# Four units at once behind the norms: the feature tile as the outer loop, with their low parts on GpSimd

## What is computed

```python
x = x + g_a[:, None, :] * rms_norm(y, attn_post_norm)
h = modulate(rms_norm(x, ffn_pre_norm), sh_f, sc_f)        # norm "x1"
u = h @ w_up                                               # the up projection, 2048 -> 2 x 5632
u = conv_b + sum(up[:, t:t + S] * conv_w[t] for t in range(3))
gate, val = split(u, 2);  y = (gelu(gate) * val) @ w_down
x = x + g_f[:, None, :] * rms_norm(y, ffn_post_norm)
h = rmsnorm(x, norm_g_2)                                   # norm "x2"
proj = h @ w_in_2                                          # the second projection, 2048 -> 48 tiles of 128
```

## Time and profile before

| | |
|---|---|
| median of three runs | 1979.6 us |
| the profiled execution's own time | 1982.76 us |
| its span | 1981.0 us |
| TensorE matmul busy | 1784.0 us, 90% of the span |
| VectorE, ScalarE, GpSimd busy | 1224.9 (62%), 855.4 (43%), 296.1 us (15%) |
| split of a half, high part, on ScalarE | 1057 ns, 512 times |
| low part of a half on VectorE | 1233 ns, 448 times |
| low part of a half on GpSimd | 2665 ns, 64 times |

### The profile page before, as it was taken

One profiled execution on the slowest core, in us unless ns is written; L12 is line 12 of the kernel. 1 busy time (PEld: TensorE's weight loads), 2 busy tenths in 40 slices (PEclk: granted clock), 3 DMA queues, 4 the chain that ended last, 5 costly groups with the idle time before them and its releaser, 6 DMA issues.

```text
span 1981.0 us, 33453 instructions
## 1 busy us (share of the span) xinstructions
PE 1784.0 (90%) x13960; PEld 1715.3 (87%) x13960; DVE 1224.9 (62%) x1745; ACT 855.4 (43%) x1384; POOL 296.1 (15%) x190
## 2 busy tenths in 40 slices
PE   1289798797997999999999999999699999988997
PEld 1289797696996999999999999999599999966797
DVE  8255788936467766766766756655654446556544
ACT  2244333453344544544544535434444443455442
POOL 8834233000443000000000000000200000042000
PEclk8589799988997999999999999999999999988999
DMA  9178768723792665766766655554245554431041
GB/s 387 71 254 318 286 242 296 264 95 117 258 344 101 232 217 194 231 211 202 230 205 214 226 191 185 176 171 163 83 142 187 183 181 160 159 118 65 25 173 59
DMA packets 102821, 377.11 MB, mean 190 GB/s; under 512 B 11536, under 2 KB 11664, under 8 KB 102544
## 3 DMA queue, kind: packets, MB, share of 16 engines
q1 hardware_dynamic: 102672, 374.99, 54.6%
HBM read 372.85 MB, written 2.10 MB: 189 GB/s over the span
## 4 chain that ended last, share of the span: by engine, by line
issue 43%; PE 39%; DVE 10%; POOL 5%; ACT 1%; DMA 1%; SPq 0%; DVEq 0%; ACTq 0%; POOLq 0%
PE ps L509 10%; PE ps L510 10%; PE ps L511 10%; POOL masks L1655 4%; DVE ada_acc L1171 3%; DVE probs L1282 1%; PE ps L540 1%; DVE stats L1256 1%; PE ps L591 1%; POOL probs L1648 1%; PE ps L547 1%; PE ps L625 1%; PE ps L610 1%; DVE w_lo L1156 1%; ACT w_hi L858 1%
## 5 line engine op out<-in xcount | busy, mean ns | idle before, releaser
L509 PE MATMUL ps<-h_hi,w_hi 128*128 128x256 f32 x3264 | 944.8, 289 | 27.4 <-DVE w_lo L1156 7.9
L510 PE MATMUL ps<-h_lo,w_hi 128*128 128x256 f32 x3264 | 931.3, 285 | 0.0
L511 PE MATMUL ps<-h_hi,w_lo 128*128 128x256 f32 x3264 | 931.0, 285 | 0.0
L1156 DVE TENSOR_TENSOR w_lo<-raw,w_hi 128x1024 fp32r<-128x1024 f32 x448 | 552.0, 1233 | 414.5 <-ACT w_hi L858 412.5
L858 ACT ACTIVATE w_hi<-raw 128x1024 fp32r<-128x1024 f32 x512 | 538.8, 1057 | 441.5 <-PE ps L511 410.7
L509 PEld LDWEIGHTS ps<-h_hi,w_hi 128*128 128x128 f32 x3264 | 633.8, 194 | 34.1 <-issue 13.4
L510 PEld LDWEIGHTS ps<-h_lo,w_hi 128*128 128x128 f32 x3264 | 634.8, 194 | 1.1
L511 PEld LDWEIGHTS ps<-h_hi,w_lo 128*128 128x128 f32 x3264 | 634.3, 194 | 0.0
L1171 DVE SCALAR_TENSOR_TENSOR ada_acc<-raw,c_act,ada_acc 128x1024 f32<-128x1024 f32 x180 | 243.0, 1381 | 0.7 <-DMA raw<-in_ada 0.4
L1661 POOL TENSOR_TENSOR w_lo<-raw,w_hi 128x1024 fp32r<-128x1024 f32 x64 | 170.1, 2665 | 439.6 <-ACT w_hi L858 439.6
L509 PE MATMUL ps<-g_hi,w_hi 128*128 128x256 f32 x704 | 200.3, 284 | 3.7 <-DVE g_lo L1492 3.7
(11 more groups left out here) (197 smaller groups left out, 1385.5 us busy)
## 6 DMA issues: line engine op xcount, KB each, us to landing
raw<-in_weights SPq DMA_DIRECT2D x512, 512.0 KB, 3.7
raw<-in_ada SPq DMA_DIRECT2D x192, 512.0 KB, 5.1
x<-in_x SPq DMA_DIRECT2D x1, 2048.0 KB, 16.4
out_y<-x SPq DMA_DIRECT2D x4, 512.0 KB, 2.7
consts<-in_consts SPq DMA_DIRECT2D x1, 863.5 KB, 6.3
params<-in_params SPq DMA_DIRECT2D x1, 589.5 KB, 4.2
probs<-in_pos_q SPq DMA_DIRECT2D x1, 128.0 KB, 2.2
probs<-in_pos_k SPq DMA_DIRECT2D x1, 32.0 KB, 1.9
```

Of the source, the lines that this page charges most:

```text
L509: nc.tensor.matmul(out, wh, hi[:, k, :], start=start, stop=False)
L510: nc.tensor.matmul(out, wh, lo[:, k, :], start=False, stop=False)
L511: last = nc.tensor.matmul(out, wl, hi[:, k, :], start=False, stop=stop)
L1156: V.tensor_tensor(w_lo[:, h % W_SLOTS, :], raw[:, raw_slot("w", h), :], w_hi[:, h % W_SLOTS, :].bitcast(F32), ALU.subtract).then_inc(lo_dv ...
```

## The change

The first four units of the up projection and of the second projection run together: h tile n is the outer loop, the four units the inner one, each in a bank of its own. The weight stream of these units is reordered on the host to fit, so a half holds two h tiles of four units, and half 0 is done only when two h tiles have met four units. The banks follow cycles of five and four in place of four and three, the tokens' transposes use other banks, and one of them waits for an earlier copy. The low parts of halves 4 to 11 of both stages go from VectorE to GpSimd. ScalarE's splits of halves 4 to 8 move in between the tiles of h_high, those of 9 to 11 behind it. The two first pairs split no halves of their own but the last one, and the `ada` items 160 and 161 go ahead of them.

```diff
+TOGETHER = 4
+def tile_at(u, n):
+    for first in (U_FF, U_IN2):
+        if first <= u < first + TOGETHER:
+            return UNIT_FIRST[first] + TOGETHER * n + u - first
+    return UNIT_FIRST[u] + n
...
+        elif U_FF <= u < U_IN2:
+            cycle, n = [0, 1, 4, 5, 2], u - U_FF
         elif U_IN2 <= u < U_CMP:
-            cycle, n = [0, 1, 5], u - U_IN2
+            cycle, n = [2, 0, 1, 5], u - U_IN2
...
 POOL_HALVES = set(range(1, N_IN, 2)) | set(range(N_IN + 1, 2 * N_IN, 2)) | set(range(H_O, H_FF, 2)) | set(
-    range(H_CMP + 2, H_OUT2 + 4))
+    range(H_FF + 4, H_FF + 12)) | set(range(H_IN2 + 4, H_IN2 + 12)) | set(range(H_CMP + 2, H_OUT2 + 4))
...
+        TOK_BANKS = [2, 3, 4, 5, 2, 3, 4, 5, 3, 4, 3]
...
+            def units_together(u, hi, lo, arriving):
+                for n in range(KT):
+                    pe.wait_ge(arriving[0], arriving[1] + n + 1)
+                    for j in range(TOGETHER):
+                        t = tile_at(u + j, n)
+                        if n == 0:
+                            bank_free(u + j)
+                        if t % TILES == 0:
+                            pe.wait_ge(*lo_done(t // TILES))
+                        product(t, ps[:, BANK[u + j], 0:S], n, hi, lo, n == 0, n == KT - 1)
...
-                        pe.wait_ge(tok_copied, i - 3)
-                    bank = SCORE + i % 4
+                        pe.wait_ge(tok_copied, i - 1 if i >= 10 else i - 3)
+                    bank = TOK_BANKS[i]
...
-            for j in range(N_IN2):
-                unit(U_IN2 + j, range(KT), h_hi, h_lo, (h_ready, HN["x2"], KT) if j == 0 else None)
+            units_together(U_IN2, h_hi, h_lo, (h_ready, HN["x2"]))
+            for j in range(TOGETHER, N_IN2):
+                unit(U_IN2 + j, range(KT), h_hi, h_lo)
...
-            def h_high(stage, shift=None, tiles=range(KT)):
+            def h_high(stage, shift=None, tiles=range(KT), ahead=None):
                 for k in tiles:
+                    if ahead is not None and k and k % 3 == 0:
+                        hi(ahead + 3 + k // 3)
...
             def ff_pair(pair, t, u):
                 h = half_of(u)
+                ahead = half_of(U_FF) + 2 * TOGETHER if pair < TOGETHER // 2 else 0
                 if t:
                     product_hi(pair - 1, t - 1)
-                hi(h + 4)
+                if not ahead:
+                    hi(h + 4)
                 center(pair, 0, u)
-                hi(h + 5)
+                if not ahead:
+                    hi(h + 5)
+                elif t == 0:
+                    hi(ahead + 3)
...
+            for h in range(H_FF + 9, H_FF + 2 * TOGETHER + 3):
+                hi(h)
...
+            for h in range(H_IN2 + 9, H_IN2 + 2 * TOGETHER + 3):
+                hi(h)
+            for j in range(TOGETHER):
+                evac(U_IN2 + j, proj2[:, j, :])
+                if j == 1:
+                    hi(H_IN2 + 2 * TOGETHER + 3)
...
+            for h in range(H_FF + 4, H_FF + 2 * TOGETHER + 3):
+                lo(h)
+                if h % 4 == 1:
+                    ada(160 + (h - H_FF - 4) // 4)
...
             nc.gpsimd.memset(y[:, :, :], 0.0).then_inc(y_zero, 1)
+            for h in range(H_FF + 4, H_FF + 12):
+                lo(h)
             scale("y2", KT, lambda k: y[:, k, :], x_ready, XN["y2"])
+            for h in range(H_IN2 + 4, H_IN2 + 12):
+                lo(h)
```

More of the change, by code:

```diff
@@ L85, with last_tile @@
     half_of(u) for u in (U_IN, U_IN_B, U_UQ, U_UKV, U_O, U_FF, U_FFL, U_IN2, U_CMP, U_OUT2))
-STEPS = sorted({f - 1 for f in UNIT_FIRST[1:]} | set(range(TILES - 1, UNIT_FIRST[-1], TILES)))
+TOGETHER = 4
[4 more added lines that the diff above has]
+    return UNIT_FIRST[u] + n
+def last_tile(u):
+    return tile_at(u, UNIT_TILES[u] - 1)
+STEPS = sorted({last_tile(u) for u in range(len(UNIT_TILES))} | set(range(TILES - 1, UNIT_FIRST[-1], TILES)))
 STEP_AT = {t: n + 1 for n, t in enumerate(STEPS)}
 def unit_step(u):
-    return STEP_AT[UNIT_FIRST[u + 1] - 1]
+    return STEP_AT[last_tile(u)]
 def half_step(h):
@@ L750, in _ @@
                 u = U_FF + FF_UNITS * g
-                for j in range(2 * FF_GROUP):
-                    unit(u + j, range(KT), h_hi, h_lo, (h_ready, HN["x1"], KT) if g == 0 and j == 0 else None)
+                if g == 0:
+                    units_together(u, h_hi, h_lo, (h_ready, HN["x1"]))
+                for j in range(TOGETHER if g == 0 else 0, 2 * FF_GROUP):
+                    unit(u + j, range(KT), h_hi, h_lo)
                 u = u + 2 * FF_GROUP
@@ L774, in _ @@
                     to_tokens(8, proj2, [VSA, VWA, VB])
+            pe.wait_ge(unit_evac, U_IN2 + N_IN2 - 3)
             pe.wait_ge(tok_copied, 11)
@@ L895, in copy_tokens @@
                     nc.scalar.activation(dst[:, t:t + 2, :].rearrange("p a b -> p (a b)"),
-                                         ps[:, SCORE + i % 4, :], ACT.Copy).then_inc(tok_copied, 1)
+                                         ps[:, TOK_BANKS[i], :], ACT.Copy).then_inc(tok_copied, 1)
             def exps(m):
@@ L1038, in _ @@
             act.wait_ge(mod_ready, N_SUMS[SH_F])
-            h_high("x1", SH_F)
+            h_high("x1", SH_F, ahead=H_FF)
             def center(pair, j, u):
@@ L1052, in ff_pair @@
                 h = half_of(u)
+                ahead = half_of(U_FF) + 2 * TOGETHER if pair < TOGETHER // 2 else 0
                 if t:
                     product_hi(pair - 1, t - 1)
-                hi(h + 4)
+                if not ahead:
+                    hi(h + 4)
                 center(pair, 0, u)
-                hi(h + 5)
+                if not ahead:
+                    hi(h + 5)
+                elif t == 0:
+                    hi(ahead + 3)
                 act.wait_ge(unit_evac, u + 1)
                 nc.scalar.activation(conv[:, 2, :], conv[:, 0, :], ACT.Gelu_apprx_tanh).then_inc(gelu_done, 1)
-                hi(h + 6)
+                if not ahead:
+                    hi(h + 6)
                 center(pair, 1, u + 1)
-                hi(h + 7)
+                if not ahead:
+                    hi(h + 7)
             def product_hi(pair, t):
@@ L1085, in _ @@
             root("x2")
-            h_high("x2")
-            for j in range(N_IN2):
+            h_high("x2", ahead=H_IN2)
+            for h in range(H_IN2 + 9, H_IN2 + 2 * TOGETHER + 3):
[4 more added lines that the diff above has]
+                    hi(H_IN2 + 2 * TOGETHER + 3)
+            for j in range(TOGETHER, N_IN2):
                 hi(H_IN2 + 2 * j + 4)
@@ L1496, in ff_pair @@
                 h = half_of(u)
+                together = pair < TOGETHER // 2
                 if t:
                     product_lo(pair - 1, t - 1)
-                lo(h + 4)
+                if not together:
+                    lo(h + 4)
                 sides(pair, 0, u)
-                lo(h + 5)
-                if item is not None:
+                if not together:
+                    lo(h + 5)
+                elif t == 0:
+                    lo(half_of(U_FF) + 2 * TOGETHER + 3)
+                if item is not None and not together:
                     ada(item)
-                lo(h + 6)
+                if not together:
+                    lo(h + 6)
                 sides(pair, 1, u + 1)
@@ L1510, in ff_pair @@
                 V.tensor_tensor(conv[:, 3, :], conv[:, 2, :], conv[:, 1, :], ALU.mult).then_inc(prod_done, 1)
-                lo(h + 7)
+                if not together:
+                    lo(h + 7)
             def add_down(u, f):
@@ L1726, in _weight_stream, with together @@
     up = _tiles(_pairs(i["w_up"][0]))
+    def together(tiles):
+        first = tiles[:TOGETHER].transpose(2, 1, 0, 3)
+        return np.concatenate([_halves(first), _halves(tiles[TOGETHER:])])
     down = i["w_down"][0]
@@ L1729, in _weight_stream @@
         n = min(FF_GROUP, FF_TILES - g)
-        parts.append(_halves(up[2 * g:2 * (g + n)]))
+        parts.append((_halves if g else together)(up[2 * g:2 * (g + n)]))
         parts.append(_halves(_tiles(down[g * P:(g + n) * P])))
@@ L1735, in _weight_stream @@
     pad = np.zeros((D, P - 24), np.float32)
-    parts.append(_halves(_tiles(np.concatenate(
+    parts.append(together(_tiles(np.concatenate(
         [kca, ksa, kwa, qa, kb[:, :64], kb[:, :64], kb[:, 64:], kb[:, 64:], qb, vca, vsa, vwa, vb, ga, pad,
```

## The result

The changed kernel takes 1984.5 us (median of 15 runs, 1981.59 to 1989.28). The kernel before, run beside it on the same chip, takes 1978.0 (15 runs, 1975.66 to 1982.14). The ratio is 1.0032 with a 95% interval of 1.0024 to 1.0040: slower by about 6.3 us (4.7 to 7.9); the medians differ by 6.5. The forecast was +6.8. I therefore compare each stage from its own first matmul.

What follows compares the result with a forecast made beforehand. TensorE was taken to bound the kernel, busy 17.00 of 17.00 us after the up projection's first unit. First stage +3.8, second +2.4 and tokens +0.6 summed to +6.8 us: median 1979.6 to 1986.4 us, range 1978 to 1991.

Steps and rivals of the forecast that it cites:

- likeliest case: GpSimd's low parts hold up VectorE's h_lo and stall TensorE in both stages; whole run +6.8 us; chance 0.60.
- TensorE's new order: First four units of both stages: gains of 3.3 and 2.8 us with nothing in the way, bank changes costing nothing.
- the rival that the order itself costs: Rival set for the experiments: TensorE's bank changes and waits in the new loop cost time themselves; no chance given.
- ScalarE's split ahead of tile 3: Half 4's split waits for half 0's slot, delaying h tile 3; stall 0.4 to 0.7 us without GpSimd's holds.
- GpSimd's holds: GpSimd's low parts delay VectorE's h_lo at tiles 3, 6, 7: stalls 2.4, 1.2, 1.5 and 2.6, 1.1, 1.4 us.
- Rival 1: In both stages the engines don't get in each other's way: sum -3.2 us, 1976.4, or -5.5, 1974.1; chance 0.15.
- Rival 3: VectorE gets two or three operations in before GpSimd, so tile 7's stalls go: about +2.9 us, 1982.5; chance 0.10.
- The disputed price: First stage: whether the first accumulations take turns with GpSimd; seventh unit 3.8 us late if so, 2.7 if not.
- The clock: Rival 2: granted clock falls behind each stage's 2.4 us stall, +3.4 us, or some 29 in all; chance 0.15.
- The prediction's own sign of being wrong: Forecast is wrong if h_lo stays 0.5 us, fifth units start before 654.9 and 1464, or clock stays 0.50 beyond 7 us.
- Half 12: Up projection's seventh unit waits 1.7 us more for half 12's low part, late behind GpSimd's holds and the convolution pairs.
- Tokens: Third token transpose waits for a copy because bank 3 is used twice: +0.6 us (bounds 0.3 and 0.9).

Runs made afterwards that it cites:

- Experiment 5: Changed kernel with low parts back on VectorE, splits three tiles later, token transposes in four banks, up projection's half 12 one convolution pair earlier: 1972.41 us, ratio 0.9962.
- experiment 1: Changed kernel with the low parts of halves 4 to 11 of both stages back on VectorE, ScalarE's order unchanged: 1975.41 us, ratio 0.9989 to the kernel before.
- experiment 2: Changed kernel with ScalarE's splits of halves 4 to 7 ahead of tiles 6, 9, 12, 15, low parts still on GpSimd: 1973.58 us, ratio 0.9975.
- experiment 6: Changed kernel with 18 unused matmuls filling TensorE's wait for h tile 3 of the up projection: 1985.92 us, ratio 1.0036 to the kernel before.
- experiment 3: Changed kernel with low parts back on VectorE and ScalarE's splits of halves 4 to 7 three tiles later: 1971.7 us, ratio 0.9967 to the kernel before.
- experiment 4: Changed kernel with the third token transpose given a bank of its own, so it waits for no copy: 1987.55 us in one execution.

## Why the prediction came out

Its likeliest case came true in its mechanism, and its sum in the main: +6.8 us forecast, +7.65 in the stages of the profiled execution, +6.3 by the ratio of the runs (4.7 to 7.9). That the sum is so near has some luck in it. It lacks 1.2 us for the clock and 0.4 in the second stage, and has 0.6 too much for half 12 and 0.1 for the tokens. Of the 1.9 us between 1984.5 and the forecast 1986.4, 1.6 are the kernel before, which is at 1978.0 in these runs and was at 1979.6 in the three that I started from.

- **TensorE's new order.** Costed at nothing for bank changes, and -3.3 and -2.8 us if h came in time. Experiment 5: -3.2 and -2.9. Right; the rival that the order itself costs has fallen. (The bound in the prediction was miscounted: a stage has 63 changes of bank, not 112, so it would take 0.05 us at each to eat its 3.3 us.)
- **ScalarE's split ahead of tile 3.** Forecast to start 5.5 us after the start and to leave a stall of 0.4 to 0.7 us by itself. It starts at 5.6 (628.78), and experiment 1 leaves 0.64 and 0.54.
- **GpSimd's holds.** Forecast stalls 2.4, 1.2, 1.5 and 2.6, 1.1, 1.4; measured 2.44, 1.05, 1.23 and 2.48, 1.09, 1.22. Shown by experiment 1, and by experiment 2 to count only where the tile is wanted at once. Rival 1 (no holds) falls with the rows of h_lo; its prices, -1.75 and -2.0, are what experiment 1 finds (-1.5 and -2.0). Rival 3 (VectorE gets several operations in) falls at tile 7, whose stall is there in both stages. Not quite right is that later holds cost nothing: in the second stage the nine tiles from tile 7 on take 13.24 us (1454.34 to 1467.58) and not 12.96, and this is most of the 0.4 us that the stage is over its forecast. Some 0.1 to 0.2 of it stand at tile 13, whose h_lo was held until 1463.10; TensorE takes it up at 1463.16, at once.
- **The disputed price.** Whether the accumulation of 0.75 us takes turns: it does (5.71 us for two), as I chose. The Trainium skill has it so (SBUF — State Buffer, section "Who interferes with whom"); and by the same section the side tap, with one operand in SBUF, doesn't: 0.47 us beside a busy GpSimd.
- **The clock.** This is the step that failed. The sum has the clock staying up behind the stall; its fall stood with the rivals, at 1.3 to 1.7 us per stage. It fell in one stage of two, for 1.2 us (experiment 6). The prediction's own sign of being wrong, a granted clock of 0.50 beyond the first 7 us of a stage, is there: 9.3 to 10.8 us after the start of the up projection. The fifth unit of the up projection is 3.5 us late: the 2.06 of the sum, this 1.2, and some 0.25 that tiles 3 to 7 are late beside it (15.13 for tile 6 in experiment 6, 14.88 in the sum). The Trainium skill (TensorE: Matmul & The Clock Gate, section "HAM oscillation — how this bites in real kernels") has the clock fall at every pass of a loop with the contraction tile outside, when TensorE waits for data in each pass; the section that the prediction names shows another loop, with a wait ahead of each matmul. The trace agrees with it only in part: the clock fell once, in one stage, behind the longest of three waits. With the waits gone the same loop keeps its clock (0.96 from 623 to 625 us in experiment 3, where it rises at 623.1, then 1.00) and gains, so the waits are at fault and not the loop.
- **Half 12.** Forecast wait 1.7 us, measured 0.68, with the clock's fall and without it (experiment 6): this chain hangs on TensorE's own pace. The seventh unit would be at 43.45 us where the sum has 44.03, so the chain was sized 0.6 too long. Inside it two errors of 2.0 and 1.4 us partly cancel: the first taps come 32.4 us after the start, or 31.2 less the clock's 1.2, and not 33.2, and the way from there took 12.2 us and not 10.8. ScalarE's rows show where the second comes from. The table load, which the forecast had ended before those taps, starts behind a split, when the taps (until 656.59) are just done:

```profile
655.72 1.06 ACT L892 ACTIVATE w_hi<-raw 128x1024 fp32r<-128x1024 f32 x1 [0.57 <-PE ps L529]
656.80 1.28 ACT L1100 ACT_TABLE_LOAD   x1
```

So the first stage is 3.8 - 0.6 + 1.2 = 4.4 us.
- **Tokens.** +0.47 against +0.6; cause shown by experiment 4.
- **The other edits.** Costed at nothing. Beside those named here no wait of TensorE is new in the trace, and experiment 5 leaves nothing of the +7.65.

## What to carry to other kernels

When an operation moves to another engine to relieve the first, look at what the first is doing just then: here a subtraction of 1.2 us taken off VectorE came back as 2.3 us of GpSimd in front of an h_lo of 0.47, at the only place where TensorE was waiting for it. When a loop is turned so that each h tile feeds four units, eight weight halves pass while the h tiles are made instead of two; their refills now share the queues with the tiles, and each has to stand behind the point where the bottleneck has released its buffer. A hold costs only where its victim is wanted at once: about the same holds cost over a microsecond each at tiles 6 and 7, nothing in the second stage once the tiles ran ahead, and 2.1 together at half 12, with the clock's fall behind it on top.

## What I had not expected of the hardware

The two engines don't take strict turns. GpSimd's low part of half 7 in the changed kernel took 4.43 us instead of 2.4 while VectorE had a stream of modulates and h_lo of 0.47 us each, one behind the other:

```profile
645.34 4.43 POOL L1723 TENSOR_TENSOR w_lo<-raw,w_hi 128x1024 fp32r<-128x1024 f32 x1 [3.27 <-ACT w_hi L892]
```

It ends at 649.77, and 2.35 us before that, at 647.4, VectorE had just run out of work (its next h_lo waits for ScalarE until 648.57). I read this as GpSimd getting in only then. At 639.67, and in the row of 254 us, GpSimd had come in after one operation of VectorE. Which of the two happens at a given boundary I can't say from these runs. It made the forecast's order of holds wrong behind tile 7, at no cost.

The second surprise is the clock behind the stalls of 2.4 us (experiment 6): back at 0.50, or 1.2 GHz, in three cases of five (and behind the 2.72 us of experiment 2), with nothing in the stall itself to tell them apart.
